# Modulation sums for the first dense stage's shift and scale: GpSimd instead of VectorE

## What is computed

```
c_act = silu(c)
mod = c_act @ ada_w[layer] + ada_b[layer]
sh1, sc1, g1, sh2, sc2, g2 = split(mod, 6)
h = rms_norm(x, norm_mix[layer]) * (1 + sc1) + sh1
x = x + g1 * mixer(h, ...)
h = rms_norm(x, norm_ffn[layer]) * (1 + sc2) + sh2
x = x + g2 * swiglu(h, ...)
```

## Time and profile before

| | us |
|---|---|
| median of 3 runs | 2085.98 (2085.65 to 2087.79) |
| profiled execution | 2083.6 |
| its span | 2081.8 |
| busy TensorE | 1980.2 (95%) |
| busy VectorE | 1660.5 (80%) |
| busy ScalarE | 1303.8 (63%) |
| busy GpSimd | 0.2 (0%), 4 instructions |

### The profile page before, as it was taken

One profiled execution on the slowest core, in us unless ns is written; L12 is line 12 of the kernel. 1 busy time (PEld: TensorE's weight loads), 2 busy tenths in 40 slices (PEclk: granted clock), 3 DMA queues, 4 the chain that ended last, 5 costly groups with the idle time before them and its releaser, 6 DMA issues. The chain is left out here.

```text
span 2081.8 us, 28079 instructions
## 1 busy us (share of the span) xinstructions
PE 1980.2 (95%) x11165; PEld 1704.3 (82%) x11165; DVE 1660.5 (80%) x2110; ACT 1303.8 (63%) x1943; POOL 0.2 (0%) x4
## 2 busy tenths in 40 slices
PE   7879999998999999999999999989999999999999
PEld 4768788877778888888888888879888789989997
DVE  5876898677689989998999899978755756757884
ACT  3644444366587777787878787757564745536663
POOL 0000000000000000000000000000000000000000
PEclk9888999999999999999999999999999999989999
DMA  8625798731269989998999899845424443324553
GB/s 322 230 101 183 268 366 336 265 147 41 102 261 367 357 334 360 363 363 324 370 357 361 332 365 363 337 166 199 143 81 140 148 160 124 120 99 143 186 187 113
DMA packets 70809, 498.76 MB, mean 240 GB/s; under 512 B 8080, under 2 KB 8336, under 8 KB 11408
## 3 DMA queue, kind: packets, MB, share of 16 engines
q1 hardware_dynamic: 69952, 494.28, 64.1%
q10 hardware_dynamic: 720, 2.62, 0.3%
HBM read 495.82 MB, written 1.05 MB: 239 GB/s over the span
## 5 line engine op out<-in xcount | busy, mean ns | idle before, releaser
L345 DVE TENSOR_TENSOR wlo<-ring,whi 128x1024 fp32r<-128x1024 f32 (+1 forms) x845 | 1016.2, 1217 | 244.1 <-ACT whi L393 223.5
L393 ACT ACTIVATE whi<-ring 128x1024 fp32r<-128x1024 f32 (+1 forms) x845 | 884.8, 1054 | 480.8 <-PE ps L237 402.9
L237 PE MATMUL ps<-whi,hT 128*128 128x256 f32 (+2 forms) x944 | 318.0, 337 | 13.0 <-DVE hTl L299 4.3
L237 PE MATMUL ps<-wlo,hT 128*128 128x256 f32 (+2 forms) x944 | 312.8, 331 | 0.0
L237 PE MATMUL ps<-whi,hTl 128*128 128x256 f32 (+2 forms) x944 | 312.7, 331 | 0.0
L237 PE MATMUL ps<-whi,xg 128*128 128x512 f32 (+1 forms) x768 | 289.3, 377 | 1.4 <-DVE wlo L345 1.1
L237 PE MATMUL ps<-whi,xgl 128*128 128x512 f32 (+1 forms) x768 | 285.8, 372 | 0.0
L237 PE MATMUL ps<-wlo,xg 128*128 128x512 f32 (+1 forms) x768 | 285.5, 372 | 0.0
L237 PE MATMUL ps<-whi,hf 128*128 128x512 f32 x528 | 208.2, 394 | 4.8 <-DVE wlo L345 3.2
L237 PEld LDWEIGHTS ps<-whi,hT 128*128 128x128 f32 x944 | 183.3, 194 | 35.1 <-DVE wlo L345 7.4
L237 PE MATMUL ps<-wlo,hf 128*128 128x512 f32 x528 | 205.7, 390 | 0.0
(11 more groups left out here) (299 smaller groups left out, 2602.8 us busy)
## 6 DMA issues: line engine op xcount, KB each, us to landing
ring<-in_wstream SPq DMA_DIRECT2D x462, 1024.0 KB, 5.0
ring<-in_wstream SPq DMA_DIRECT2D x4, 832.0 KB, 5.2
modrow<-in_gates ACTq DMA_DIRECT2D x3, 512.0 KB, 6.9
ring<-in_wstream SPq DMA_DIRECT2D x6, 256.0 KB, 2.6
cst<-in_cst SPq DMA_DIRECT2D x1, 1028.0 KB, 7.7
x<-in_x SPq DMA_DIRECT2D x1, 1024.0 KB, 13.6
work<-in_bias ACTq DMA_DIRECT2D x2, 512.0 KB, 5.2
ring<-in_wstream SPq DMA_DIRECT2D x2, 512.0 KB, 3.8
```

The source lines that it names most:

```text
L237: i = self.e.matmul(out, lhsT, rhs, start=start, stop=stop, skip_group_check=True)
L345: i = self.e.tensor_tensor(K.wlo[:, q % NS, 0:cols], src, hi.bitcast(F32), ALU.subtract)
L393: i = self.e.activation(K.whi[:, q % NS, 0:cols], K.ring[:, m % RING, at:at + cols], ACT.Copy)
```

## The change

GpSimd gets a program of its own. It waits for `cact`, for the transposes of the latent keys and for the end of the stick-breaking work on VectorE, and then works through the eight slots: for each block a multiply (`tensor_scalar`) by the column of `cact`, in place in the ring (for k = 0 straight into the sum), and for k > 0, after a wait on its own semaphore, an addition (`tensor_tensor`) to the sum. That makes 16 multiplies and 14 additions. The ring slots of these two slices are freed by GpSimd. VectorE's 16 block steps go. TensorE's sum of the first slice moves to ahead of the eighth chunk of the output projection (PSUM bank 7), that of the second to behind the projection (bank 6); both biases and the scale product move behind the residual on VectorE. The second layer's mixer has no such sums and keeps its order. The diff, cut to its core (creation of the semaphore and the registration of the new program left out):

```diff
+class Pool(Unit):
+    def __init__(self, K, e):
+        super().__init__(K, e, K.pool, [K.pool])
+
+    def ts(self, out, a, s, op, key=None):
+        inc = self.done.up(key)
+        if self.e is not None:
+            self.e.tensor_scalar(out, a, s, None, op).then_inc(self.done.sem, inc)
+
+    def tt(self, out, a, b, op, key=None):
+        inc = self.done.up(key)
+        if self.e is not None:
+            self.e.tensor_tensor(out, a, b, op).then_inc(self.done.sem, inc)
...
-def dve_amid(K, v, n0, n1):
-
-    for n in range(n0, n1):
-        accumulate(K, v, K.amid[n // 2], (n % 2,))
+def pool_sums(K, g):
+
+    g.wait_ge(K.act, "cact")
+    g.wait_ge(K.pe, (("m0", "mkT"), "t", 6))
+    g.wait_ge(K.dve, ("m0", SB[1], "log"))
+    for m in K.amid:
+        _, _, idx, blocks = K.plan[K.slots[m]]
+        acc = sums_of(K, SUMMED.index((idx[0], blocks[0][1] // 1024)))
+        g.wait_ge(K.full[m % RING], 16 * (m // RING + 1))
+        for j, (k, _, _) in enumerate(blocks):
+            w, c = K.ring[:, m % RING, 1024 * j:1024 * j + 1024], K.cact[:, k:k + 1]
+            g.ts(w if k else acc, w, c, ALU.mult, key=None)
+            if k:
+                g.wait_ge(K.pool, K.pool.n)
+                g.tt(acc, acc, w, ALU.add, key=("acc", m) if j == len(blocks) - 1 else None)
...
+def column_bank(n):
+    return 6 if n == 2 else 7
+
+
 def pe_accsum(K, pe, n):
-    pe.wait_ge(K.dve, ("acc", K.acc_last[n]))
+    pe.wait_ge(K.pool if n in AMID else K.dve, ("acc", K.acc_last[n]))
...
-    pe.take(7)
+    b = column_bank(n)
+    pe.take(b)
     for j in range(8):
-        pe.mm(K.ps[7][:, j:j + 1], sums_of(K, n)[:, 128 * j:128 * j + 128], K.cst("ones")[:, 0:1], True, True,
+        pe.mm(K.ps[b][:, j:j + 1], sums_of(K, n)[:, 128 * j:128 * j + 128], K.cst("ones")[:, 0:1], True, True,
               done=("accsum", n) if j == 7 else None)
-    pe.given(7, (K.dve, ("keep", n)))
+    pe.given(b, (K.dve, ("keep", n)))
...
@@ pe_mixer
     values(4)
-    if l == 0:
-        pe_accsum(K, pe, 1)
     turn(5)
     values(5)
     turn(6)
-    if l == 0:
-        pe_accsum(K, pe, 2)
     values(6)
...
-    pe_rows(K, pe, f"out{l}", hrows(K), KT, block=ready(K, pe, (s, "o")))
+    pe_rows(K, pe, f"out{l}", hrows(K), KT, block=ready(K, pe, (s, "o")), at_part=lambda n: pe_accsum(K, pe, 1) if n == 7 and l == 0 else None)
+    if l == 0:
+        pe_accsum(K, pe, 2)
...
@@ dve_mixer
     weights(3)
     values(0)
     turn(1)
-    amid(1)
     weights(4)
-    amid(1)
     values(1)
-    amid(1)
     values(2)
     turn(3)
     weights(5)
-    amid(3)
     values(3)
-    amid(2)
     turn(4)
     weights(6)
-    amid(4)
     values(4)
     turn(5)
-    amid(2)
     values(5)
-    amid(2)
-    if l == 0:
-        dve_keep(K, v, 1)
...
     turn(6)
-    if l == 0:
-        dve_keep(K, v, 2)
...
-    dve_mod_scale(K, v, l, 3, f"nf{l}")
+    if l:
+        dve_mod_scale(K, v, l, 3, f"nf{l}")
     dve_residual(K, v, f"out{l}", KT, K.gate1 if l else K.gate, f"nf{l}")
+    if l == 0:
+        dve_keep(K, v, 1)
+        dve_keep(K, v, 2)
+        dve_mod_scale(K, v, l, 3, f"nf{l}")
...
@@ Kernel.order_weights
-                self.last_use[m] = (self.dve, ("acc", m))
+                self.last_use[m] = (self.pool if n in AMID else self.dve, ("acc", m))

```

More of the change, by code:

```diff
@@ L607, in dve_keep @@
         return
-    v.tt(K.mod[:, layer, 8 * g:8 * g + 8], K.ps[7][:, 0:8], K.col(f"ab{layer}", 8 * g, 8), ALU.add, key=("keep", n))
+    v.tt(K.mod[:, layer, 8 * g:8 * g + 8], K.ps[column_bank(n)][:, 0:8], K.col(f"ab{layer}", 8 * g, 8), ALU.add, key=("keep", n))
 def act_gate_bias(K, a, n):
@@ L1533, in values @@
         dve_values(K, v, s, x, js[x])
-    done = [0]
-    def amid(n):
-        if l == 0:
-            v.wait_ge(K.pe, ((s, "mkT"), "t", 6))
-            dve_amid(K, v, done[0], done[0] + n)
-            done[0] += n
     ahead(6)
@@ L2875, in vector_program, with pool_program @@
     K.dve.here("end")
+def pool_program(K, g):
+    pool_sums(K, g)
 def sync_program(K, sp):
@@ L2918, in __init__ @@
         self.pe, self.act, self.dve, self.sp = signal("pe_done"), signal("act_done"), signal("dve_done"), None
+        self.pool = signal("pool_done")
         self.hi, self.lo = signal("high_split"), signal("low_split")
@@ L2922, in __init__ @@
         self.s_bias, self.s_out, self.s_gates = signal("bias"), signal("stored"), signal("gate_biases")
-        self.signals = [self.pe, self.act, self.dve, self.hi, self.lo, *self.full]
+        self.signals = [self.pe, self.act, self.dve, self.pool, self.hi, self.lo, *self.full]
         self.counted, self.bank = False, {}
@@ L3111, in build @@
         scalar_program(K, Scalar(K, None))
+        pool_program(K, Pool(K, None))
         K.begin(True)
@@ L3129, in _ @@
             scalar_program(K, Scalar(K, e))
+        @block.gpsimd
+        def _(e):
+            pool_program(K, Pool(K, e))
 def pack_stream(inputs):
```

## The result

The changed kernel takes 2100.64 us (median of 4 runs, 2095.73 to 2102.0) against 2085.82: a ratio of 1.0065, 95% interval 1.005 to 1.0079. It is slower by 14.8 us; I had forecast 10.5 us less. The profiled execution took 2101.1 us, span 2099.3.

The account below looks back on a forecast made before the run. VectorE's order of work, with modulation sums between attention steps, was taken to bound the first mixer's attention. Attention -22.0, contention +7.7 and moves +3.8 gave -10.5 us: 2075.5 us median, range 2066.5 to 2084.5.

Parts of the forecast that it names:

- the price of GpSimd's multiply: GpSimd's slice sums: each 128x1024 multiply taken as 1.1 us, after ScalarE's plain pass of 1.06 us.
- the sum: Forecast total: GpSimd's work 49.8 us; attention -22.0, contention +7.7, moved TensorE work +3.8, giving -10.5 us.
- The range of 30 to 77 us for GpSimd: All 30 GpSimd instructions: low end at VectorE's times, high end at 2.57 us each, twice VectorE's slower row.
- signs that the prediction is wrong: ScalarE waiting for a projection ring load, GpSimd averaging over 2 us, or first dense matmul shifting under 7 or over 15.
- The rival of late weights: Output-weight loads behind GpSimd's slots: at 77 us weights land at 201, chunk starts near 204; +7.4 us, 2093.4; chance 0.10.
- the moves: TensorE's two sums over partitions, moved to the output projection and behind it: 1.9 us each, 3.8 us added.
- The attention: From stick-breaking's end (A, 118.7) to the output projection's first matmul (B): B at 160.7 instead of 182.68, 22.0 us less.
- Contention: 11 VectorE instructions on the path each wait half a GpSimd instruction, 0.8 us: 7.7 us added before the first projection matmul.
- The rival of whole-instruction blocking: VectorE's 11 instructions each wait a whole GpSimd instruction, the first half; total -4.4 us, 2081.6; chance 0.22.

Follow-up runs that it names:

- the run with the other form of the multiply: Changed kernel with GpSimd multiplying by a tensor_tensor whose second operand is the cact column repeated, instead of a tensor_scalar: 2085.99 us, ratio 1.0004.
- narrow work on GpSimd: Changed kernel with GpSimd working on 32 of 1024 columns: 2922 us, not readable; with the rest of both sums zeroed, 2065.64 us, ratio 0.9908.
- the run with ScalarE's share: Changed kernel with seven of the 16 multiplies on ScalarE, GpSimd's others as tensor_tensor with a repeated column: 2077.9 us, ratio 0.9964.
- the contention run: Changed kernel narrowed to 32 columns, rest zeroed, plus 14 GpSimd additions of 1024 columns on unread data behind the sums: 2075.07 us, ratio 0.995.

## Why the prediction was wrong

**The step that failed is the price of GpSimd's multiply.** "I take ScalarE's plain pass over one tensor, 1.06 us, as nearest for the multiply (1.1)": it took 2.85 us. The 16 multiplies cost 28 us more than the sum had; the additions (2.3 taken) had 2.35 alone and 2.45 on average. The range of 30 to 77 us for GpSimd did not reach the 80.8 that it took. I named the multiply as dear as an addition unlikely; it was dearer. GpSimd's instructions averaged 2.66 us, and ScalarE waited for a ring load: both were named as signs that the prediction is wrong.

**What waits for it was named rightly, with one wait missed.** The rival of late weights, at 0.10, is what happened: SP waited 91.5 us for GpSimd's slots in eight waits. For 77 us it gave +7.4; for 80.8 us that would be about 11. A to C measured +15.3. The rest is two steps I did not have.

The first is a bank. The projection's third group of columns needs banks 0 and 1 back from the residual of the first group, and VectorE does that residual behind the splits of the last two chunks in its order. So the last load held not only its own chunks but the bank: TensorE waits 5.2 us for `aux` until 209.65, after the load landed at 204.0. By the rival's own 3 us from landing to chunk it would have begun near 207, so the bank costs some 2.6 us. Where the load lands 8 us earlier, in the run with the other form of the multiply, TensorE waits 0.8 us for `aux`. VectorE in the changed kernel:

```profile
205.13 2.36 DVE L345 TENSOR_TENSOR wlo<-ring,whi 128x1024 fp32r<-128x1024 f32 x2 [4.92 <-ACT whi L408]
207.41 0.68 DVE L292 TENSOR_TENSOR aux<-ps,gate 128x512 f32<-128x512 f32 x1
...
208.85 0.69 DVE L292 TENSOR_TENSOR aux<-ps,gate 128x512 f32<-128x512 f32 x1
```

The second is the clock. Behind those 5.2 us without a product it is granted 0.52 from 209.6 to 214.7 us, the 1.2 GHz level, and the chunk's 24 products start 0.21 us apart; in the kernel before, products of this shape start 0.12 us apart. That is 2.2 us. As an estimate from these numbers, 11 + 2.6 + 2.2, less 0.6 that the moves cost under my 3.8, makes 15.2.

**The attention was right.** Replayed 42.0 us from A to B; with narrow work on GpSimd it was 41.7, and 43.3 where the clock fell between 126 and 130 us. At the gap that I shortened (134 to 143 us) the clock stayed at 1.00; the fall ahead of it, 1.6 us, the replay did not have, and the changed kernel has it too. That the changed kernel's own A to B is 62.7 is the first load, issued at 166.3 and landed 15.7 us after ScalarE asked for it.

**The moves were right in price**, 3.8 taken and 3.2 measured, of which the sum over the first slice is 1.84 us.

**Contention was too small.** I took half an instruction for each of 11 steps, 7.7 us, of which 4.5 for the first seven. With additions back to back it measured 8.3 us when they ended before the last four steps, and 12.2 us (22.4 less 10.2) in the run with ScalarE's share, where they did not. The rival of whole-instruction blocking had 13.8 us there, which is nearer to the measured 12.2 than the sum's 7.7. In the changed kernel itself the tail met multiplies more than additions, and the late weights had made it late already. A step that started 0.08 us after a multiply waited 1.05 us and ended 1.86 us before it:

```profile
152.75 2.99 POOL L367 TENSOR_SCALAR ring<-ring,cact 128x1024 f32<-128x1024 f32 x1
```

```profile
151.92 0.88 DVE L299 SCALAR_TENSOR_TENSOR r_t<-ssq,sd 128x4 f32<-128x4 f32 x1
152.83 1.05 DVE L299 SCALAR_TENSOR_TENSOR r_t<-r_t,sd 128x4 f32<-128x4 f32 x1
153.91 0.16 DVE L299 SCALAR_TENSOR_TENSOR rs<-r_t,sd 128x4 f32<-128x4 f32 x1
```

The same again at 177.04, 1.05 us behind a multiply that began at 176.97. So an addition mostly holds VectorE off for its whole length, a multiply by a scalar in these two cases for about 1 us of its 2.85. Why it lets go is not shown. The Trainium skill, SBUF — State Buffer, Who interferes with whom, says that the second to issue waits for the whole instruction of the first: the additions agree with it (2.25 us behind one of 2.35), this multiply does not. The Trainium skill, GPSIMD Engine Reference, Engine selection, calls a one-input operation there roughly line-rate and a two-input one about twice as slow as VectorE; the addition agrees, 2.35 us against 1.23 on VectorE, but the order is reversed, 2.85 us for the multiply by a scalar against 0.75 on VectorE, and the measurement decides.

Not settled: the profiled executions put 8.3 us of the contention run's 9.4 on these steps; the other 1.1 lie within the spread of the runs (2071.0 to 2076.04, against 2063.77 to 2068.58).

## What to carry to other kernels

Before work goes to an engine whose trace has no such instruction, measure each kind of instruction by itself. My high end was twice VectorE's slower instruction, 2.57 us, and the multiply took 2.85; one form of it cost up to 50% more than another with the same result. If the moved work holds ring slots, its total length is the latency of the loads behind it, so compare that with when the next stage asks, not with idle time. And count the instructions with two SBUF operands that the other engine runs meanwhile on the path: behind an addition a step of 0.16 us then costs up to the whole instruction that it meets.

## What I had not expected of the hardware

GpSimd's multiply by a scalar is slower than its product of two tensors: 2.85 us (2.77 with a constant) against 1.89 with one column repeated (2.05 on average in the kernel, held up by VectorE) and 2.35 for two full tensors, all over 1024 columns. With 32 columns they take 0.36 and 0.25 us, so the scalar form costs 2.5 ns a column. ScalarE does the same multiply in 1.14 us.
